# Small matmuls of constants in TensorE's waits, in a two-layer trunk of mixer and expert layers

## The reference, cut to what is computed

```python
for l in range(DEPTH):
    mod = (c_act @ w_ada[l] + b_ada[l])[:, None, :]
    shift1, scale1, gate1, shift2, scale2, gate2 = jnp.split(mod, 6, axis=-1)
    h = rmsnorm(x, norm1_g[l]) * (1.0 + scale1) + shift1
    u = h @ w_in[l]                                   # 1024 x 3072
    ...
    x = x + gate1 * (y_mix @ w_out[l])
    h2 = rmsnorm(x, norm2_g[l]) * (1.0 + scale2) + shift2
    x = x + gate2 * hier_moe(h2, ...)                 # 16 experts, 1024 x 256 x 1024
```

## Time and profile before

| | us |
|---|---|
| median of 3 runs | 628.68 (627.68 to 630.69) |
| the profiled execution | 629.93 |
| its span, first to last instruction | 628.1 |
| TensorE's mean granted clock | 0.949 |
| busy in the span: TensorE matmuls | 553.2 (88%) |
| busy in the span: VectorE, ScalarE, GpSimd | 282.7 (45%), 218.8 (35%), 17.0 (3%) |
| DMA, mean over the span | 301 GB/s from HBM |

### The profile page before, as it was taken

The page is one execution under the profiler, slowest core; times in us unless marked ns, Lnnn a source line. Parts: engine busy times, 40 slices in busy tenths (PEclk is TensorE's granted clock), DMA queues, the critical chain, the costliest instruction groups (busy, mean ns, idle before and its releaser), DMA issues.

```text
span 628.1 us, 7864 instructions
## 1 busy us (share of the span) xinstructions
PE 553.2 (88%) x3140; PEld 355.2 (57%) x3140; DVE 282.7 (45%) x495; ACT 218.8 (35%) x379; POOL 17.0 (3%) x74
## 2 busy tenths in 40 slices
PE   3797999869799999999949999986976899999993
PEld 1566899455656534444327899944664644444331
DVE  4516890964266022222377389196326502222233
ACT  2415533641044422221145453364105432232120
POOL 3004000000000000000000000000000000000000
PEclk9898999979798999999987999997978799999998
DMA  8999943891599999999997644299069089999951
GB/s 312 388 387 369 360 158 129 335 423 47 210 417 411 379 386 416 414 412 415 402 387 290 216 143 160 101 365 410 30 229 373 8 288 380 416 413 413 413 213 69
DMA packets 51726, 189.77 MB, mean 302 GB/s; under 512 B 4618, under 2 KB 4698, under 8 KB 44260
## 3 DMA queue, kind: packets, MB, share of 16 engines
q1 hardware_dynamic: 50464, 185.62, 75.9%
q0 software_dynamic: 896, 2.45, 1.1%
q10 hardware_dynamic: 324, 1.13, 0.5%
HBM read 188.12 MB, written 1.06 MB: 301 GB/s over the span
## 4 chain that ended last, share of the span: by engine, by line
PE 77%; DVE 13%; ACT 5%; issue 2%; DMA 1%; DVEq 0%; SPq 0%; ACTq 0%
PE ps L1492 18%; PE ps L1307 11%; PE ps L1291 11%; PE ps L1518 9%; PE ps L1396 6%; PE ps L1472 6%; PE ps L1532 5%; PE ps L1206 4%; DVE wlo L758 3%; PE ps L1237 1%; DMA raw<-in_w_ada_dram 1%; DVE cbc L974 1%; PE ps L1386 1%; ACT whi L490 1%; ACT work L606 1%
## 5 line engine op out<-in xcount | busy, mean ns | idle before, releaser
L758 DVE TENSOR_TENSOR wlo<-raw,whi 128x1024 fp32r<-128x1024 f32 x64 | 75.0, 1221 | 19.3 <-ACT whi L490 19.1
L490 ACT ACTIVATE whi<-raw 128x1024 fp32r<-128x1024 f32 x64 | 64.8, 1054 | 27.1 <-PE ps L1291 8.7
L1492 PE MATMUL ps<-raw,qkT 128*64 128x512 f32 x256 | 58.3, 597 | 1.6 <-ACT work L709 1.6
L1518 PE MATMUL ps<-raw,work 128*64 128x512 f32 x256 | 58.0, 598 | 0.0
L1492 PE MATMUL ps<-raw,cbc 128*64 128x512 f32 x256 | 57.2, 594 | 0.0
L1147 DVE SCALAR_TENSOR_TENSOR work<-ps,cw,work 128x256 f32<-128x256 f32 x16 | 10.9, 684 | 102.7 <-ACT work L703 102.7
L1206 PE MATMUL ps<-raw,c_rep 128*32 128x512 f32 x384 | 46.0, 616 | 10.8 <-DMA raw<-in_w_ada_dram 10.8
L1307 PE MATMUL ps<-act_hi,whi 128*128 128x256 f32 x192 | 54.5, 284 | 0.0
L1307 PE MATMUL ps<-act_hi,wlo 128*128 128x256 f32 x192 | 54.3, 283 | 0.0
L1307 PE MATMUL ps<-act_lo,whi 128*128 128x256 f32 x192 | 54.3, 283 | 0.0
L1136 DVE TENSOR_TENSOR v_sb<-ps,gates 128x512 f32<-128x512 f32 x32 | 22.1, 691 | 64.6 <-PE ps L1518 64.6
(11 more groups left out here) (227 smaller groups left out, 842.2 us busy)
## 6 DMA issues: line engine op xcount, KB each, us to landing
raw<-in_w_ada_dram SPq DMA_DIRECT2D x40, 1024.0 KB, 8.5
raw<-in_w_gate_dram SPq DMA_DIRECT2D x64, 512.0 KB, 7.6
raw<-in_w_up_dram SPq DMA_DIRECT2D x64, 512.0 KB, 9.5
raw<-in_w_down_dram SPq DMA_DIRECT2D x32, 1024.0 KB, 11.4
raw<-in_w_in_dram SPq DMA_DIRECT2D x24, 1024.0 KB, 14.5
raw<-in_w_ada_dram SPq DMA_DIRECT2D x16, 512.0 KB, 11.7
raw<-in_w_out_dram SPq DMA_DIRECT2D x8, 1024.0 KB, 5.2
gates<-gate_line POOLq DMA_DIRECT2D x2, 1024.0 KB, 6.4
```

Source lines behind the costliest of these rows:

```text
L490: act.activation(whi[:, slot(n), :], raw[:, r, (i % 2) * 1024:(i % 2 + 1) * 1024], ACT.Copy).then_inc(hi_done, 1)
L758: dve.tensor_tensor(wlo[:, slot(n), :], raw[:, ring_slot[("w", l, i // 2)], (i % 2) * 1024:(i % 2 + 1) * 1024], whi[:, slot(n), :].bitcast ...
L1492: ins = pe.matmul(ps[i * SLOTS:(i + 1) * SLOTS, 0, :], hg[p // 2 % 2][:, k, c0:c0 + SLOTS], ws[i][:, :, kk, :], start=(k == 0), stop=(k == ...
L1518: ins = pe.matmul(ps[i * SLOTS:(i + 1) * SLOTS, 2 + n, :], hidT[:, p % 2, kk, i * SLOTS:(i + 1) * SLOTS], ws[i][:, c0:c0 + 512], start=(kk ...
```

## The change

A helper `spin(bank, n)` issues n float32 matmuls of the 128 by 128 tile `ones` by the stationary `ident`, into the first 128 columns of a bank, without a semaphore. It is called at five places: 20 times ahead of the first wait for weights (the wait for the constants is moved ahead of it), 4 ahead of the first transposes, 12 behind `first_cols(0)`, 32 ahead of layer 1's first transposes (bank 1), and 10 in layer 1's second norm, where layer 0 has a part of the next modulation. All but the fourth write bank 5. No other engine's program is changed, and nothing is taken out.

```diff
+            def spin(bank, n):
+
+                for _ in range(n):
+                    pe.matmul(ps[:, bank, 0:P], ident[:, :], ones[:, :], start=True, stop=True)
+
+            pe.wait_ge(const_ready, 2)
+            spin(5, 20)
             pe.wait_ge(rowsel_ready, 1)
             pe.wait_ge(crep_ready, 2)
             ada_acc("A0", 0, range(0, 1))
-            pe.wait_ge(const_ready, 2)
             pe.wait_ge(lines_in, 16 * NLINES)
...
             ada_acc("A0", 0, range(1, 2))
+            spin(5, 4)
             transposes(0)
             ada_acc("A0", 0, range(2, 4))
             first_cols(0)
+            spin(5, 12)
             for l in range(L):
                 n0 = HALVES * l
                 if l > 0:
+                    spin(1, 32)
                     transposes(2 * l)
...
                 if l + 1 < L:
                     ada_acc("A", l + 1, range(0, 4))
+                else:
+                    spin(5, 10)
                 pe.wait_ge(row_added, 4 * l + 4)
                 transposes(m)
```

## The result

| | before | after |
|---|---|---|
| median, us (15 runs each) | 628.68 (627.10 to 630.73) | 631.28 (629.06 to 639.10) |
| ratio after to before | | 1.0044, 95% interval 1.0026 to 1.0061 |
| the profiled execution, us | 629.93 | 630.93 |
| its span, us | 628.1 | 629.0 |
| TensorE's mean granted clock | 0.949 | 0.949 |

The forecast was 622.2 us. The change costs 2.6 us, and TensorE's mean clock in the profiled execution is what it was. One of the 15 executions after, the one of 639.10, ran in a slower state and is left out of the ratio.

A forecast was written before the change was run, and what follows sets the result against it. TensorE's own pace (77% of the chain) and the norms it waits for were taken as the bound; 3.7 + 2.4 + 0.4 = 6.5 us off the profiled 629.93 gave 623.4, median 622.2, forecast 620 to 624.5, range 618.5 to 626.5.

The forecast's parts named there:

- The branch: Between the layers, TensorE's branch on overflow ahead of the 32 spins: hidden behind the last matmuls, no delay (0 to 0.5 us).
- the 2.4 that were to be won: Between the layers, 32 spins: 0.95 from transposes plus 1.6 from first matmuls, less 0.15 late, 2.4 us gained.
- Rival D: Spins between the layers run at half clock behind the branch and overshoot, the start's 20 also at half: 631 us, chance 0.05.
- A spin's price: One dummy fp32 matmul: 0.25 us at full clock (0.22 to 0.27), 0.46 at half.
- The start, by its steps: Spins end at 10.6 us, first projection starts at 25.0 for 27.14, its first 24 matmuls take 5.71 for 7.33.
- The start, by its size: Start and first projection: 2.1 us from earlier work plus 1.6 from the projection's pace, 3.7 in all (0.9 to 3.8).
- moves with the rest, as does the half clock behind it: The 3.29 us wait for VectorE at 53.83 us, and the half clock behind it, shift along with the earlier start.
- The second norm: Layer 1's second norm, 10 spins: clock kept through 481.5 us or nothing, about even odds, 0.4 us gained (0 to 1.0).
- Rival C: The loads bind the start, the projection waiting for w_in, so the start gives 0.5 us: 625.3 us, chance 0.09.
- Rival A: Transposes don't hold the clock, at the start or between the layers; the sum is 2.4 us: 626.3 us, chance 0.07.
- F: Half clock behind 53.83 us and in 489 to 495 falls away too, 2 to 4 us more: 619 us, chance 0.12.
- The Trainium skill's rule of one half of the time at half clock: Penalty is half the time at half clock: 9.5 us over the stretches the spins bear on, 619 us.

The follow-up runs named there:

- x2_only32: The kernel before plus only the 32 matmuls ahead of layer 1's first transposes: 633.68 us, ratio 1.0066.
- y6_start: The kernel before plus the three groups at the start (20, 4 and 12 matmuls) and nothing else: 627.05 us, ratio 0.9976.
- y1_12alone: The kernel before plus only the 12 matmuls behind the first modulation columns: 628.50 us, ratio 0.9994.
- y1_again: The kernel of y1_12alone run once more for a second profile: 626.23 us (one run).
- x1_no32: The changed kernel without the 32 matmuls between the layers, the others kept: 626.68 us, ratio 0.9966 to the kernel before.
- x3_short: The changed kernel with TensorE's unrun code for overfull experts cut from 16 experts to one, the branch kept: 622.49 us, ratio 0.9904.
- z1_all: z2_between plus small matmuls in the waits that the change had left, in both layers: 611.87 us, ratio 0.9735.
- z2_between: The changed kernel with 9 matmuls of 512 columns ahead of the branch for the 32, and 6 small behind layer 1's first transposes: 629.70 us, ratio 1.0017.
- z4_nine: z2_between without the 6 small matmuls behind layer 1's first transposes: 626.19 us, ratio 0.9967.
- y5_6alone: The kernel before plus only 6 matmuls behind the first modulation columns: 627.71 us, ratio 0.9992.
- y2_20alone: The kernel before plus only the 20 matmuls ahead of the first weights and 4 ahead of the first transposes: 628.06 us, ratio 1.0001.

## Why the prediction was wrong, point by point

- **The branch** is the step that failed: "TensorE's sequencer can do it while the last eight matmuls run. I take no delay from it (0 to 0.5)". It took 6.08 us. The estimate went by the same branch on VectorE (about 1 us), which jumps over little code. No row of the trace before shows the gap, since it ended 2.3 us ahead of the wait for VectorE. The term was +2.4 and measured -4.9 (x2_only32; -4.1 by its ratio). By medians the 32 cost 631.28 - 626.68 = 4.6 us inside the change. With the 2.4 that were to be won that is 7 of the 9.1 us between forecast and result; the start's size, below, is the other 2.
- **Rival D** named the place and the mechanism (spins that start behind the branch, and the clock with them), at 0.05. It priced a spin at half clock for all 32; they took 8.92 us in all, since the clock rose at 329, and the loss was 4 to 5 us all the same. "Against: TensorE is dense right up to 322.2, so the clock is full when they start" was wrong through the 6 us of idleness ahead of them. Its 631 is the measured 631.28 by luck: it adds 6.9 us of delay (measured: 4.5, 334.60 for 330.09) to a start held to about 2 us by spins at half clock, and these ran as forecast.
- **A spin's price** was right: 0.25 forecast; 7.38/32 = 0.23 at full clock. At half it was a little dear: the 14 instructions that start in the 3 us from 326 are 0.21 each, 0.43 a spin, for 0.46.
- **The start, by its steps**: spins to 10.6 (10.7), first projection at 25.0 (24.89), 24 matmuls in 5.7 (5.72). Held by w_in's first unit, as the chain of the changed kernel says (15.12 us of that DMA from 6.22).
- **The start, by its size**: 3.7 forecast, 1.5 measured (y6_start 0.9976, interval 0.9963 to 0.9989). The mis-sized step is in the sum: "it is 1.25 above the median ..., so the median would be 622.2". It took a gain read from one execution off a median. The profiled execution of before (629.93) has the clock at half in 28 to 30 and in 325 to 338; others of the same kernel took from 626.7 to 631.2 us, and where the clock changes in them wasn't profiled. Against the profiled execution the term held: in y6_start's the 24 matmuls of the second block begin at 32.92 for 36.32, 3.4 us earlier, and 629.93 - 3.7 = 626.2 stands beside its 626.13. That is partly luck, since the one lies 1.25 above its median and the other 0.9 below. Against the median the term was more than twice too large. Why isn't shown; that the half-speed stretches differ from one execution to the next (y1_12alone and y1_again) means that a stretch seen in one profile isn't there to be won in each.
- **The gain is not kept whole downstream**: in the changed kernel's profile the second block of line 1300 started 3.85 us earlier (49.98 for 53.83) and took 19.42 for 18.25, since the clock was at half from 49.2 to 56.0 (before: 54.9 to 58.3). "moves with the rest, as does the half clock behind it" left out that it can come back longer. It needn't: y6_start, the same program up to there, took 18.22.
- **The second norm**: 0.4 forecast; x1_no32 (0.9966) and y6_start (0.9976) differ by the 10 and can't be told apart. In the changed kernel's profile the second eight transposes took 1.09 us for 1.96; in x1_no32's, with the same 10, 1.93. Of the nine profiles with these 10 five have the short time, so even odds was about right.
- **Rival C** (loads) fell: behind the first unit of w_in TensorE's chain has no wait for the weights in layer 0's projection. **Rival A** (transposes don't hold the clock, as the Trainium skill has it, TensorE: Matmul & The Clock Gate, Part 4: PE-mode transpose) is refuted for these fp32 transposes. In x3_short, whose windows stand below, the clock is 1.00 throughout with 1.97 us of transposes in the middle, though matmuls and spins stand around them. And in y1_again, whose windows stand behind them, TensorE did nothing but its sixteen transposes (324.59 to 328.27) between the last scatter at 316.75 and the projection at 329.44, and the clock was back at 1.00 before the projection began. The trace doesn't agree with the page. It isn't sure to rise, though: in the kernel before it stayed at 0.50 behind the same sixteen. **F** didn't come in the change; what it names came in z1_all, another kernel: the other half-speed stretches go only if their own waits are filled.
- The Trainium skill's rule of one half of the time at half clock (the same page, Terms): a mean clock of 0.949 over 628.1 us is 64 us at half, one of 0.991 over 609.6 us (z1_all) is 11. Half of the difference is 26.5 us; the median fell by 16.7 (628.61 to 611.87). The trace doesn't agree. One reason is that TensorE was idle in part of that time: in the stretches at half it was busy for 46.5 us before and for 6.7 in z1_all, and half of that difference is 19.9. The other 3 us aren't accounted for, and the half clock at the start, ahead of the first recorded change, is in none of these figures.

The windows of x3_short:

```profile
318.00:326.00 8.00, 7.81 (x67) 7.40 (x65) 7.78 (x11) 2.98 (x5) 0.00 (x0) 1.00 1.05 386
326.00:330.00 4.00, 2.17 (x18) 1.74 (x17) 2.27 (x5) 2.10 (x5) 0.00 (x0) 1.00 1.05 386
330.00:336.00 6.00, 5.75 (x25) 4.80 (x26) 5.90 (x10) 5.45 (x8) 0.00 (x0) 1.00 0.56 172
```

and of y1_again:

```profile
317.00:324.00 7.00, 0.00 (x0) 0.00 (x0) 6.78 (x10) 2.09 (x4) 0.00 (x0) 0.86 1.05 385
324.00:328.00 4.00, 3.41 (x16) 3.27 (x16) 1.36 (x3) 0.91 (x3) 0.00 (x0) 0.50 1.05 387
328.80:329.40 0.60, 0.00 (x0) 0.00 (x0) 0.60 (x2) 0.60 (x3) 0.00 (x0) 1.00 1.06 389
```

## What to carry to other kernels

Dummy matmuls in TensorE's waits pay when they end before the wait would have ended and stand in nearly every wait ahead of dense work: 78 of them in some of the waits cost 0.4%, z1_all's in nearly all waits won 2.65%. Before filling an idle stretch ask what the engine's sequencer does in it: a branch over long code can hide 6 us of no issue in a wait of 8. Matmuls behind such a branch come too late; ahead of it few long ones leave it unhindered and many short ones don't. And a gain read from one execution, where the clock steps at places that differ from one to the next, is to be taken off that execution and not off the median.

## What the runs showed of the hardware

- A not-taken body of four to sixteen experts' code on TensorE cost 6.0 to 6.3 us without issue behind it while DMA moved 386 GB/s, 3.18 us while it was nearly idle, and 0.19 us with one expert's code. The difference between the first two lies ahead of the packet of the instruction queue (3.75 and 0.99 us from the branch to it).
- Code behind such a jump can be late a second time, by 1 to 3 us (2.87 us in z2_between, 0.95 in z4_nine).
- 128 small instructions ahead of the branch keep the sequencer from it; 32 instructions of about the same total time don't (7.31 and 7.03 us of matmuls, 5.47 and 0 us of issue left over).
- Sixteen fp32 transposes of 128 by 128, and nothing else, were followed by a rise of the clock to full (y1_again; y5_6alone and y2_20alone have it too); in the kernel before the same sixteen weren't.
- Executions of one kernel differ by 5 us and more (y1_12alone: three at 624.8 to 625.0, nine at 627.3 to 629.6, at mean clocks of 0.938 to 0.951; z4_nine: 622.66 to 629.69). Their stretches at half clock differ too; what decides between them stays open.
